# Value tiles projected by token, a new order of layer 1 and earlier first loads in a three-layer transformer kernel

## What is computed

```python
h = rms_norm(x, attn_norm_w[layer]); u = h @ w_in[layer]
# layer 0: q, k, v, g from u;  o = rms_norm(retention(q, k, v)); o_main = silu(g) * o
# layer 1: q, k normalized per head; v from u
a = p[:, :, 0] - lam * p[:, :, 1]                     # two softmax maps of a head
o = einsum('bhij,bjhe->bihe', a, v); o_main = rms_norm(o, diff_subln_w) * (1 - lambda_init)
# both: memory attention, mkv = rms_norm(mem) @ w_mem_kv[layer]
o_mem = memory_attention(rms_norm(qc), rms_norm(mk), mv)
x = x + concatenate([o_main, o_mem], -1) @ w_out[layer]
h = rms_norm(x, ffn_norm_w[layer]); gu = h @ w_gate_up[layer]
x = x + (silu(gu[..., :FFN_DIM]) * gu[..., FFN_DIM:]) @ w_down[layer]
# layer 2: z, xbc, dt, q, k, v, f = h @ w_in_2;  y_ssd = ssd_mixer(...), y_fox = fox_mixer(q, k, v, f)
```

## Time and profile before

| | us |
|---|---|
| median of 3 runs | 1123.24 |
| lowest, highest | 1116.76, 1123.5 |
| the profiled execution | 1124.99 |
| its span | 1123.2 |
| granted clock, mean of the span | 0.982 |

### The profile page before, as it was taken

One profiled execution on the slowest core, in us unless ns is written; L12 is line 12 of the kernel. 1 busy time (PEld: TensorE's weight loads), 2 busy tenths in 40 slices (PEclk: granted clock), 3 DMA queues, 4 the chain that ended last, 5 costly groups with the idle time before them and its releaser, 6 DMA issues.

```text
span 1123.2 us, 24024 instructions
## 1 busy us (share of the span) xinstructions
PE 1069.1 (95%) x8706; PEld 1028.5 (92%) x8706; DVE 767.4 (68%) x1323; ACT 591.9 (53%) x1063; POOL 172.4 (15%) x186
## 2 busy tenths in 40 slices
PE   6999999999999879799999999989999999999999
PEld 5989999999999778689999999989788999999998
DVE  5865686666556876775666557867777669999843
ACT  6654564444544544464444545655455556666532
POOL 3100121111110001031111110001111014444400
PEclk9999999999999998989999999999899999999999
DMA  7533455555665222335555665443232255555563
GB/s 264 183 122 108 130 177 181 183 187 172 184 188 169 95 85 83 115 128 181 181 184 177 184 183 168 159 144 121 88 112 87 85 207 172 185 187 180 156 214 106
DMA packets 50904, 174.45 MB, mean 155 GB/s; under 512 B 5648, under 2 KB 6928, under 8 KB 50704
## 3 DMA queue, kind: packets, MB, share of 16 engines
q1 hardware_dynamic: 50832, 173.46, 47.4%
HBM read 172.39 MB, written 1.05 MB: 154 GB/s over the span
## 4 chain that ended last, share of the span: by engine, by line
PE 81%; DVE 13%; ACT 3%; issue 2%; POOL 1%; DMA 1%; SPq 0%; DVEq 0%; ACTq 0%; POOLq 0%
PE bank L640 24%; PE bank L641 24%; PE bank L642 24%; DVE ring_lo L1384 3%; DVE xw_lo L1390 1%; PE bank L729 1%; DVE tmp L1501 1%; PE bank L820 1%; PE bank L853 1%; PE bank L743 1%; PE bank L840 1%; ACT tmp L1148 1%; PE bank L800 1%; PE bank L918 1%; DVE negmax L1624 1%
## 5 line engine op out<-in xcount | busy, mean ns | idle before, releaser
L640 PE MATMUL bank<-xw_hi,ring_hi 128*128 128x256 f32 x1736 | 499.8, 288 | 3.7 <-ACT lam L1284 1.1
L641 PE MATMUL bank<-xw_lo,ring_hi 128*128 128x256 f32 x1736 | 492.0, 283 | 0.0
L642 PE MATMUL bank<-xw_hi,ring_lo 128*128 128x256 f32 x1736 | 491.8, 283 | 0.0
L1384 DVE TENSOR_TENSOR ring_lo<-ring_raw,ring_hi 128x1024 fp32r<-128x1024 f32 (+1 forms) x336 | 400.1, 1194 | 55.2 <-ACT ring_hi L972 49.5
L972 ACT ACTIVATE ring_hi<-ring_raw 128x1024 fp32r<-128x1024 f32 (+1 forms) x336 | 340.8, 1017 | 92.2 <-PE bank L642 84.5
L640 PEld LDWEIGHTS bank<-xw_hi,ring_hi 128*128 128x128 f32 x1736 | 333.9, 192 | 11.8 <-issue 6.2
L641 PEld LDWEIGHTS bank<-xw_lo,ring_hi 128*128 128x128 f32 x1736 | 334.0, 192 | 0.2
L642 PEld LDWEIGHTS bank<-xw_hi,ring_lo 128*128 128x128 f32 x1736 | 333.7, 192 | 0.0
L640 PE MATMUL bank<-act_hi,ring_hi 128*128 128x256 f32 x784 | 228.0, 291 | 14.8 <-DVE ring_lo L1764 8.8
L641 PE MATMUL bank<-act_lo,ring_hi 128*128 128x256 f32 x784 | 225.1, 287 | 0.0
L642 PE MATMUL bank<-act_hi,ring_lo 128*128 128x256 f32 x784 | 225.0, 287 | 0.0
(11 more groups left out here) (175 smaller groups left out, 918.6 us busy)
## 6 DMA issues: line engine op xcount, KB each, us to landing
ring_raw<-w_up SPq DMA_DIRECT2D x132, 512.0 KB, 3.2
ring_raw<-w_in SPq DMA_DIRECT2D x85, 512.0 KB, 3.3
ring_raw<-w_down SPq DMA_DIRECT2D x48, 512.0 KB, 3.6
ring_raw<-w_down SPq DMA_DIRECT2D x24, 384.0 KB, 3.9
ring_raw<-w_oa SPq DMA_DIRECT2D x16, 384.0 KB, 3.0
ring_raw<-w_kv SPq DMA_DIRECT2D x8, 512.0 KB, 6.6
ring_raw<-w_ob SPq DMA_DIRECT2D x8, 512.0 KB, 3.3
ring_raw<-w_oa SPq DMA_DIRECT2D x8, 512.0 KB, 3.6
```

The lines of the kernel that those rows point to most:

```text
L640: mm(bank[b][:, 0:T], w_hi, tile(hi, t), start=kk == 0, stop=False)
L641: mm(bank[b][:, 0:T], w_hi, tile(lo, t), start=False, stop=False)
L642: last = mm(bank[b][:, 0:T], w_lo, tile(hi, t), start=False, stop=end)
L1384: V.tensor_tensor(ring_lo[:, a:b], ring_raw[:, a:b], ring_hi[:, a:b].bitcast(f32), SUB).then_inc(lo_done, 1)
```

## The change

Three things. First, the value tiles (24 in all) are projected by token: the activations' halves of 128 tokens are stationary and the weight block moves, six matmuls with 128 columns for a block. The result already has tokens on the partitions; DVE evacuates it straight into x_tok or v_tok, scaled by rstd_tok, the two columns of rstd turned by two small transposes once for each input stream (`root_by_token`, on PE after tile 2 of `in` and after tile 3 of kv). The turns of these tiles are gone. Second, layer 1 has another order of tiles and another plan, its norms alternate between banks 4 and 7, and the output projection is cut 4 + 4 inputs in place of 6 + 2. Third, at the start the parameters come in two loads (56 columns first) and the first weight tile in two halves, and ACT's squares of the memory stream stand later.

```diff
-          ("in1", 20, [8], 20), ("oa1", 8, [6], 8), ("ob1", 2, [8], 2), ...
+          ("in1", 20, [8], 20), ("oa1", 8, [4], 8), ("ob1", 4, [8], 4), ...
...
-         "in1": [18, 19] + [t for j in range(3) for t in (2 * j, 2 * j + 1, 6 + 2 * j, 7 + 2 * j, 12 + 2 * j, 13 + 2 * j)],
+         "in1": [18, 19, 0, 1, 6, 7, 2, 3, 8, 9, 12, 13, 4, 5, 10, 11, 14, 15, 16, 17],
...
+    for t, slot in ((18, 2), (0, 3), (6, 5), (2, 7), (8, 9), (4, 13), (10, 15), (8 + 64, 20)):
+        norm(1, slot, t)
+    norm(1, 16, 6 + 64, True)
+    norm(1, 23, 10 + 64, True)
...
+    for h, slots in enumerate(((9, 10, 11, 12), (11, 12, 13, 14), (13, 14, 15, 18), (15, 16, 17, 19),
+                               (18, 19, 20, 21), (20, 21, 21, 22))):
+        first, soft, turned, last = slots
...
+    for k, slot in ((6, 11), (7, 11), (0, 19), (1, 19), (2, 23), (3, 23), (4, 26), (5, 26)):
+        at(1, slot, "mix", k)
...
+                    if by_token(ph, c):
+                        for tt in range(2):
+                            x_hi, x_lo = (buf[:, t * T + tt * P:t * T + (tt + 1) * P] for buf in (hi, lo))
+                            o = bank[b][:, tt * P:(tt + 1) * P]
+                            mm(o, x_hi, w_hi, start=kk == 0 and tt == 0, stop=False)
+                            mm(o, x_hi, w_lo, start=False, stop=False)
+                            last = mm(o, x_lo, w_hi, start=False, stop=end and tt == 1)
+                        continue
...
+            def root_by_token(q):
+
+                pe.wait_ge(rstd_done, q + 1)
+                for tt in range(2):
+                    last = nc.tensor.transpose(bank[5][:, 16 * tt:16 * tt + 16], rstd[0:16, tt * P:(tt + 1) * P],
+                                               con[0:16, CCOL["ident"]:CCOL["ident"] + 16])
+                last.then_inc(rt_ps, 1)
...
+                    if name[:2] in ("kv", "in") and c == (3 if name == "kv" else 2):
+                        root_by_token(q)
...
+            def root_by_token():
+
+                n = root_count[0] = root_count[0] + 1
+                dve.wait_ge(rt_ps, n)
+                V.tensor_copy(rstd_tok[:, :], bank[5][:, 0:32:16]).then_inc(rt_out, 1)
+                dve.wait_ge(rt_out, n)
...
+            def evac_by_token(layer, t, ps):
+                dst, c0 = BY_TOKEN[layer, t]
+                V.tensor_tensor(dst[:, :].rearrange("p (t c) -> p t c", t=2)[:, :, c0:c0 + P],
+                                ps.rearrange("p (t c) -> p t c", t=2),
+                                rstd_tok[:, :].unsqueeze(2).to_broadcast([P, 2, P]), MUL).then_inc(out_ready, 1)
...
-            for m in range(2):
-                stream_square(0, m, u)
-            act.wait_ge(w_loaded[0], 16)
-            for half, done in ((0, first_hi), (1, hi_done)):
+            for half, loaded, done in ((0, half_loaded, first_hi), (1, w_loaded[0], hi_done)):
+                act.wait_ge(loaded, 16)
...
```

More of the change, by code:

```diff
@@ L208, in mem_pairs @@
                 at(layer, slot, "scores", "mem", 2 * pair + n, 0)
-    for n, t in enumerate((22, 23, 26, 27)):
-        at(0, n, "turn", t)
     for h in range(RET_HEADS):
@@ L217, in plans @@
     mem_pairs(0)
-    for n, slot in enumerate((5, 6, 9, 10, 13, 14)):
-        at(0, slot, "turn", 6 + n)
     for j, slot in enumerate((10, 12, 14)):
@@ L501, in roots_of, with by_token, norm_bank @@
             return normed(n)[:, 0:P]
+        def by_token(ph, c):
+            if ph.name == "kv":
+                return c % 4 >= 2
+            return ph.name[:2] == "in" and (int(ph.name[2]), ORDER[ph.name][c]) in BY_TOKEN
+        def norm_bank(n):
+            first = min(number["norm", k] for _, k in number if type(k[0]) is str and k[1] == 1 and _ == "norm")
+            count_ = sum(1 for _, k in number if type(k[0]) is str and k[1] == 1 and _ == "norm")
+            return bank[7 if 0 <= n - first < count_ and (n - first) % 2 else 4]
         def norm_no(layer, t):
@@ L697, in ffn_ready @@
                 return lambda k: pe.wait_ge(ffn_lo, FT * layer + k + 1)
-            issued = {"norm": 0, "turn": 0, "weights": 0, "pair": 0}
+            issued = {"norm": 0, "turn": 0, "weights": 0, "pair": 0, "root": 0}
             def bank4_free():
@@ L719, in norm @@
                 for d in range(4):
-                    last = mm(bank[4][32 * d:32 * d + 32, 0:P], cmat(SPEC[layer, t][0], 32),
+                    last = mm(norm_bank(n)[32 * d:32 * d + 32, 0:P], cmat(SPEC[layer, t][0], 32),
                               normed(n)[:, d * P:(d + 1) * P], start=True, stop=True)
@@ L1103, in roots @@
                 act.wait_ge(np_ms, n + 1)
-                A(y, bank[4][:, 0:width], ACT.Ln, scale=scale, bias=eps(e)).then_inc(np_ln, 1)
+                A(y, norm_bank(n)[:, 0:width], ACT.Ln, scale=scale, bias=eps(e)).then_inc(np_ln, 1)
                 act.wait_ge(np_ln, n + 1)
```

111 lines of the change are left out of this document (63 added, 48 removed), and 2 rows, old and new, of the table PHASES.

## The result

The changed kernel takes 1180.91 us, the median of four runs (1180.37 to 1182.37), against 1122.01 for the kernel before in four runs beside it (1116.76 to 1123.5). The ratio is 1.0524, with a 95% interval of 1.0478 to 1.0569. That is 58.9 us slower. The forecast was 31.1 us slower, 1154, with 1134 to 1174 as its range; the sign was right, and the time lies 7 us outside the range.

The account below looks back on a forecast made before the run. PE's own time was taken to bound the kernel. Terms 59.9 - 3.9 - 2.4 - 5 - 14.5 - 3 = +31.1 us on 1124.99 gave 1156.1, at the median's level 1154 us, 2.8% slower; range 1134 to 1174.

Parts of the forecast that it names:

- the three terms of the tiles: The 24 by-token tiles: more load and matmul pairs +59.9, turns saved net -3.9, turns' waits for bank 5 -2.4 us.
- What bounds the kernel, and the count: Whole kernel: PE's own time bounds it, 81% of the chain; 9242 matmul records expected after the change.
- The load holds the pair, 0.112 us: By-token tiles: each pair with 128 moving columns is held by its weight load, 0.112 us, 5.4 us a tile.
- the first two rivals: The 24 tiles: load doesn't hold the pair, 0.06 us, 1094 us (4%); loads partly overlap, 0.086 us, 1124 us (4%).
- The term of the tiles, +59.9: The 24 by-token tiles: 1152 pairs at 0.112 us replace 576 at 0.120 us, +59.9 us.
- if PEclk falls in the stretches that hold the new tiles: By-token stretches: a sign named beforehand that would show the forecast wrong, a drop of TensorE's clock there.
- The third rival: By-token tiles: they bring the clock down, 3.4 us at half clock in each of 11 groups, 17.5 us, 1172 us; 12%.
- The saved turns, -6.3 with the bank waits: The 24 tiles' turns go: net -3.9 us of PE time, and -2.4 us of waits for ACT to empty bank 5.
- The start, -5: Kernel start: earlier first matmul 1.0, earlier second tile 2.0, less half clock 2.0, together -5 us; bounds 0 and -7.
- Late next is the sum of squares: Kernel start: POOL would begin the sum of squares later and be the next thing late; no size given.
- Layer 1, -14.5, and layer 2, -3: Layer 1's new order: waits -9, clock -5.5 us; layer 2's long tiles cover waits before L729 and at L918, -3 us.
- The fourth and fifth rivals: Layer 1's order only moves waits, 1169 us (10%); start, layer 1 and layer 2 gain their bounds, 1135 us (8%).

Follow-up runs that it names:

- paired: The changed kernel with value tiles taken in pairs, one stationary token half for two ring tiles' weights (256 moving columns); 1108.06 us, ratio 0.9855.
- both_waits_gone: The changed kernel with kv's mean of squares one ring tile later and layer 1's tile 4 norm spread one slot later; 1142.82 us, ratio 1.0154.
- tokens_old_order: The kernel before with only the value tiles projected by token, in the old order and with the old start; 1170.31 us, ratio 1.0451.
- start_only: The kernel before with only the new start: parameters in two loads, first weight tile in halves, squares later; 1122.19 us, ratio 0.9986.
- kv_later_mean: The changed kernel with kv's mean of squares taken on PE after ring tile 2 in place of tile 1; 1170.66 us, ratio 1.0438.
- order_without_tokens: The changed kernel with all 24 value tiles projected by feature again and turned, new order and start kept; 1106.64 us, ratio 0.9858.
- one_wide_tile: The changed kernel, waits left, with only layer 1's value tile 14 projected by feature again and turned; 1159.22 us, ratio 1.0298.

## Why the prediction was wrong, point by point

Two of the runs split the change in two, so the sum can be held against them at the level of the medians. The order and the start took 16.0 us off (1122.62 less 1106.64), where the terms of start and layer 1 had -19.5. The tiles added 74.3 us on top of that (1180.91 less 1106.64), where the three terms of the tiles and that of layer 2, which rests on the long tiles and is absent without them, had 59.9 - 3.9 - 2.4 - 3 = +50.6. Of the miss of 27.2 us between these medians 23.7 are the tiles' and 3.5 the rest's.

- **What bounds the kernel, and the count.** Right. 9242 matmuls, PE the chain, DVE's and ACT's work beside it worth nothing.
- **The load holds the pair, 0.112 us.** Right at full clock: starts 0.11 us apart, a tile of 48 pairs 5.3 us. paired bears the reason out: twice the columns a load, 0.12 us. So the first two rivals (0.06 and 0.086 us) are out. The Trainium skill, "TensorE: Matmul & The Clock Gate", section "Back-to-back issue gap", with its 81 ns a matmul for a stream with 128 columns, does not fit these fp32r loads; the measured 110 ns decides.
- **The term of the tiles, +59.9.** This is the step that failed. It was summed with one duration, that of full clock, for all 1152 pairs. 240 of them ran at 0.21 us, which adds 23.5 us, the size of the tiles' miss. Taking both waits away returned 38.1 us, which has in it the waits' own length and the ordinary work that ran at half clock beside these pairs. The sign for it was named, "if PEclk falls in the stretches that hold the new tiles", and it came.
- **The third rival.** It had the right effect and the wrong mechanism, and so the wrong size. I looked for tiles that bring the clock down, and charged one stretch of 3.4 us in each of 11 groups, 17.5 us. No group does that at full clock (all 24 tiles at 1.00 in both_waits_gone). What happened is that half clock came at a wait, as it did in the earlier trace rows, and did not end while the tiles behind it ran: two stretches of 27.3 and 41.0 us. I had noticed that these pairs' loads outlast their matmuls and asked only about the fall, not the recovery. The half-clock stretch of the earlier trace rows, from 446.4, lasts 3.4 us and had ordinary tiles behind it; what would stand there in the new order was the question to ask.
- **The recovery.** In the kernels before and after, stretches without by-token tiles had full clock back after 3.4 or 6.8 us, and the one with three by-token tiles after 41.0 us, 40.53 of them busy. The Trainium skill, "TensorE: Matmul & The Clock Gate", section "What's actually happening", says that activity releases the throttle. The trace agrees for the ordinary tiles and disagrees for the by-token ones, during which nothing was released though PE was busy without a gap.
- **The saved turns, -6.3 with the bank waits.** Not measured apart. tokens_old_order, at +47.7, is 5.9 below the 53.6 of the three terms together (2.9 below, with layer 2's -3), within what its own spread of 14 us allows.
- **The start, -5.** Wrong: -1.05 by start_only, not to be told from 0. "Late next is the sum of squares" was named in the prediction and given no price. It costs PE 2.7 us, and in the changed kernel the half clock behind it too: kv_later_mean returns 10.3 us. A new wait that is named needs a number.
- **Layer 1, -14.5, and layer 2, -3.** Right in substance: order_without_tokens has 16.0 us for layer 1 and the start together. The waits of layer 1 came to 9 us ("near 11"). In layer 2 of the changed kernel the wait of 3.3 us stays, as said, the total at its line fell from 5.7 to 4.3 us, and that at the norm roots from 2.8 to 0.8: 3.4 us, for a term of 3. What I missed is that a wait which "stays" in the slots 9 to 15, 3.4 us at the spread of tile 4, is priced by what stands behind it. "The clock of its first stretch above 0.97" was right up to 448.6 (1.00) and wrong from there (0.50).
- **The fourth and fifth rivals** did not come: order and start together gain 16.0 us, neither nothing nor their bounds.

What stays open is why full clock did not come back under these tiles. In the two long stretches it never came back inside a by-token tile, and it did 4.9 and 3.0 us into an ordinary one (the changed kernel's kv, one_wide_tile). But full clock came back behind 3.5 us of attention steps, with 128 and 256 columns, at the end of the stretch of 41.0 us, and in tokens_old_order a stretch that ran into a by-token tile (419.9 to 423.3) ended after 3.4 us, most of it other work. Which property of the by-token pairs matters, no run separates. Open too is what makes the clock fall: a wait of about 3 us stands before both long stretches, but not every such wait does it. This one, in layer 2 of order_without_tokens, has a granted clock of 1.00 around it (735 to 750):

```profile
741.66 0.87 PE L1007 MATMUL bank<-tmp,x_tok 128*64 128x256 f32 x8 [3.32 <-DVE tmp L1806]
```

**A version that beats both.** order_without_tokens (1106.64, 1.4% faster than before) and paired (1108.06) can't be told from each other. The order is what gains, and by-token projection costs nothing that can be told once two tiles share a load, but it doesn't gain either: the little time of PE that the turns took came back as longer waits.

## What to carry to other kernels

Before you swap the stationary and the moving operand, count the loads: where the weight load holds the pair, halving the moving columns all but doubles the time of a tile (5.3 us against 2.9), and widening them to 256 again (two weight tiles side by side) takes that back. Price a wait of TensorE by what runs behind it: 3.4 us of waiting before tiles of short matmuls cost some 22 us here, the same wait before one ordinary tile 5. When a change keeps a wait and moves new work behind it, look at the granted clock there first, both how it falls and how it comes back.

## What the runs showed of the hardware that I had not expected

- At half clock PE can be busy without a gap for 41.0 us (40.53 us busy) and stay at a granted clock of 0.50. Of its 198 matmuls there 144 were by-token pairs with 128 moving columns and 54 were attention steps between them.
- The same tiles at full clock leave it there: ten of them within 129.7 us at 1.00.
- One tile of 24 pairs with 256 columns in place of 48 with 128, at the right place, is worth some 20 us (19.7 in layer 1), although by its own pairs it is worth 2.5.
- Starts of pairs with 128 columns are 0.21 us apart at half clock and 0.11 at full clock; their load records last 0.33 and 0.19 us. Pairs with 256 columns are 0.21 and 0.12 us apart, so at half clock the two kinds cost the same.
- Waits of 3.3 us don't always bring half clock: at L1007 of order_without_tokens (741.66) the clock stayed at 1.00.
- A moving operand that takes its 256 columns from two ring slots by a stride costs the same 0.12 us a pair as one that lies in one piece.
